# One modulation piece among every three weight pieces, in a slot of its own, and four modulation sums moved to the attention's output

## The chip, the cores and the metric

The kernel runs on one core of a Trainium2 chip. The metric is device time in microseconds of one execution, the median of several runs. The engines are TensorE (PE; its weight loads are shown apart as PEld), VectorE (DVE), ScalarE (ACT), GpSimd (POOL) and SyncE (SP), which only issues DMAs here.

## What is computed

A chain of transformer blocks on 256 tokens of width 1024, all in float32. Only the first block is touched here:

```python
mod = jax.nn.silu(c) @ w_ada[l] + b_ada[l]
sh1, sc1, g1, sh2, sc2, g2 = jnp.split(mod, 6, axis=-1)
h = modulate(rms_norm(x, norm1_g[l]), sh1, sc1)
x = x + g1[:, None, :] * token_mixer(h, w_in[l], ...)   # retention and dilated attention, gated, times w_o
h = modulate(rms_norm(x, norm2_g[l]), sh2, sc2)
x = x + g2[:, None, :] * squared_relu_mlp(h, w_ff1[l], w_ff2[l])
```

`c` is one vector of 1024, so `mod` is one row of six vectors of 1024: the scale and shift of the first norm (vectors 1 and 0), the gate of the mixer (2), the shift, scale and gate around the MLP (3, 4, 5). `w_ada` is 1024 x 6144 float32, 4 MB for each vector. The first two vectors are wanted before the first matrix product, the other four only after the mixer's last product. Behind this block come a second kind of block, twice, with mixture-of-experts layers.

## The kernel before

**Weights.** Every matrix is cut into units of 128 x 1024 float32 (512 KB). SP brings two units at a time, a piece of 1 MB, into `w_raw`, a ring of 8 unit slots, which are 4 piece slots, each with its own semaphore `raw_landed`. To keep float32 precision, ACT rounds a unit into `w_hi` (`hi`, L622), POOL takes the difference into `w_lo` (`lo`, L581, two half units of 512 columns each), and PE multiplies three times: high by high, low by high, high by low (`mm3`, L1058 to L1060). `w_hi` and `w_lo` have 4 unit slots: ACT may write unit k only when PE has used unit k-4 (`unit_used`). A unit costs PE 12 matmuls of 512 columns. Once POOL has made the difference of a unit it counts `lo_ready`, and the raw slot is free for SP.

**The stages.** Four units make a tile of the input projection (`up`, 256 tokens x 512 columns in two PSUM banks, alternately `G` and `AC`). Tiles 0 to 3 are queries and keys of the retention, 4 to 7 values, 8 to 11 its gate, and one more (`U_ATT_FIRST`, units 48 to 51) the first attention tile. While PE runs these, DVE rotates tiles 0 to 3 (`rotate`, L1854 to L1860), copies tiles 4 to 7, multiplies scores with the decay (`decayed`), normalises the four heads (`group_norm`, L1877 to L1892) and gates them (`gated`, L1897). PE puts its transposes (L1202) and the heads' scores and outputs (L1211 to L1223) between the tiles. Then comes the retention's output product (`down_pairs`, units 52 to 67, in eight pairs q with a transposition and its rounding in front of each), the attention's tiles (units 68 to 115) with the heads between units, the attention's output (116 to 119), the mixer's output (`U_WO`, 120 to 127) and the MLP (from 128).

**Modulation.** A vector of `mod` is made from 8 raw slots of `w_ada`: `ada(i, s0, s1)` has DVE multiply slot s with a column of silu(c) and add it to 128 partial rows, one SCALAR_TENSOR_TENSOR of 128 x 1024 per slot (L1802), and count `ada_used`. The sum over partitions is one product with ones on PE (`mod_sums`, L1184, into both banks of `G`), copied back by ACT (`mod_rows`, L682). In the stream, `ADA_BEFORE = (0, 0, 2, 4, 5, 8)` puts each vector as a whole round of 8 slots: vectors 0 and 1 of the order at the start, then one round before the weight rounds 2, 4, 5 and 8, that is before units 16, 32, 40 and 64. SP's loop waits, piece by piece, for `ada_used` or `lo_ready` of what stood in that slot, and issues the next. DVE works the rounds off between its other steps: vector 2 between the rotations, 3 and 4 between the group norms, 5 in the retention's output, where PE also makes the four sums (before pairs 4 to 7, `ret_head`).

**Order.** Each engine runs its own program in order; an engine waits at a semaphore and everything behind it waits too. That holds for SP's issues as well.

The trace numbers used below: a unit's steps are L622 (ACT), L581 (POOL) and L1058 to L1060 (PE).

## Time and profile before

| | before |
|---|---|
| median of 3 runs | 1512.55 us (1509.37 to 1516.2) |
| profiled execution | 1514.78 us, span 1513.0 us |
| PE busy | 1351.1 us (89%) |
| DVE busy | 854.0 us (56%) |
| ACT busy | 728.2 us (48%) |
| POOL busy | 633.0 us (42%) |
| HBM read | 274.66 MB, 184 GB/s over the span |

Busy time is how long instructions of an engine ran. The chain that ended last follows the work back from the end: an engine with a large share there is what the time hangs on in that stretch, even if its busy share over the whole span is small. POOL's 42% over the span is such a case: it makes the differences in the first half, and DVE makes them in the expert layers.

### The profile page before, as it was taken

The numbers are of one execution on the slowest core, as the hardware profiler recorded it, in microseconds if no ns is written. First come the engines' busy times: TensorE is split into PE (matmuls) and PEld (weight loads), VectorE is DVE, ScalarE is ACT, GpSimd is POOL, SyncE is SP. The second block draws the span as 40 slices with busy tenths as digits, with TensorE's granted clock in tenths as the row PEclk, the third lists the DMA queues.
The fourth block names the chain that finished last, engine by engine and source line by source line (L and its number), as shares of the span: only waits on it lengthen the run. The fifth ranks groups of instructions, "written<-read, shape, count | busy, mean of one in ns | idle before, by whom it ended". The sixth has DMA issues, their size and how long they took to land.

```text
span 1513.0 us, 18663 instructions
## 1 busy us (share of the span) xinstructions
PE 1351.1 (89%) x6112; PEld 1091.0 (72%) x6112; DVE 854.0 (56%) x1334; ACT 728.2 (48%) x1069; POOL 633.0 (42%) x525
## 2 busy tenths in 40 slices
PE   6979879999998799997987978999979888699995
PEld 2768667788876588885776767888757767678884
DVE  7463963222244543115656657777756745677777
ACT  4323354444563344443555425666635653266664
POOL 2777789787668589995300230000060024000000
PEclk8999999999998799998998878999989978699998
DMA  9765567654443445453531007778733300277782
GB/s 386 302 246 195 199 231 244 260 179 149 143 150 139 148 170 194 172 189 111 195 112 56 1 1 266 295 289 321 287 141 139 112 0 1 105 289 290 295 314 84
DMA packets 44199, 279.98 MB, mean 185 GB/s; under 512 B 5421, under 2 KB 8749, under 8 KB 11726
## 3 DMA queue, kind: packets, MB, share of 16 engines
q1 hardware_dynamic: 37138, 263.82, 47.3%
q10 hardware_dynamic: 6974, 15.05, 2.9%
q8 instruction: 48, 0.79, 0.2%
q14 instruction: 39, 0.32, 0.1%
HBM read 274.66 MB, written 4.19 MB: 184 GB/s over the span
## 4 chain that ended last, share of the span: by engine, by line
PE 39%; issue 31%; POOL 25%; DVE 3%; DVEq 1%; ACT 0%; POOLq 0%; ACTq 0%
POOL w_lo L581 23%; PE G L1058 6%; PE G L1060 6%; PE G L1059 6%; PE AC L1058 5%; PE AC L1060 5%; PE AC L1059 5%; POOL arena L606 1%; PE AC L1631 1%; PE T L1660 1%; PE G L1184 0%; DVEq L1752 0%; PE T L1274 0%; PE AC L1284 0%; DVE w_lo L1725 0%
## 5 line engine op out<-in xcount | busy, mean ns | idle before, releaser
L581 POOL TENSOR_TENSOR w_lo<-w_raw,w_hi 128x512 fp32r<-128x512 f32 (+1 forms) x488 | 608.7, 1282 | 443.2 <-ACT w_hi L622 435.8
L622 ACT ACTIVATE w_hi<-w_raw 128x1024 fp32r<-128x1024 f32 x448 | 471.1, 1059 | 412.7 <-PE G L1060 193.1
L1725 DVE TENSOR_TENSOR w_lo<-w_raw,w_hi 128x1024 fp32r<-128x1024 f32 x230 | 278.2, 1223 | 64.2 <-ACT w_hi L622 56.1
L1058 PE MATMUL G<-w_hi,xT_hi 128*128 128x512 f32 x432 | 181.9, 421 | 28.1 <-POOL w_lo L581 19.4
L1058 PE MATMUL AC<-w_hi,yT_hi 128*128 128x512 f32 x480 | 192.6, 401 | 9.8 <-POOL w_lo L581 3.9
L1059 PE MATMUL AC<-w_lo,yT_hi 128*128 128x512 f32 x480 | 189.3, 394 | 0.0
L1060 PE MATMUL AC<-w_hi,yT_lo 128*128 128x512 f32 x480 | 188.9, 393 | 0.0
L1060 PE MATMUL G<-w_hi,xT_lo 128*128 128x512 f32 x432 | 174.6, 404 | 0.0
L1059 PE MATMUL G<-w_lo,xT_hi 128*128 128x512 f32 x432 | 174.3, 404 | 0.0
L1058 PE MATMUL G<-w_hi,arena_r 128*128 128x512 f32 x320 | 128.0, 400 | 3.9 <-DVE arena L2519 3.2
L1058 PE MATMUL AC<-w_hi,xT_hi 128*128 128x512 f32 (+1 forms) x288 | 118.0, 410 | 13.2 <-DVE xT_lo L1732 7.6
L1060 PE MATMUL G<-w_hi,arena_r 128*128 128x512 f32 x320 | 125.1, 391 | 0.0
L1059 PE MATMUL G<-w_lo,arena_r 128*128 128x512 f32 x320 | 124.7, 390 | 0.0
L1058 PEld LDWEIGHTS G<-w_hi,xT_hi 128*128 128x128 f32 x432 | 85.2, 197 | 50.1 <-POOL w_lo L581 13.3
L1058 PEld LDWEIGHTS AC<-w_hi,yT_hi 128*128 128x128 f32 x480 | 92.4, 193 | 31.7 <-POOL w_lo L581 6.6
L1060 PE MATMUL AC<-w_hi,xT_lo 128*128 128x512 f32 (+1 forms) x288 | 112.8, 392 | 0.0
L1059 PE MATMUL AC<-w_lo,xT_hi 128*128 128x512 f32 (+1 forms) x288 | 112.8, 392 | 0.0
L1060 PEld LDWEIGHTS AC<-w_hi,yT_lo 128*128 128x128 f32 x480 | 92.1, 192 | 19.7
L1059 PEld LDWEIGHTS AC<-w_lo,yT_hi 128*128 128x128 f32 x480 | 92.5, 193 | 18.3
L1060 PEld LDWEIGHTS G<-w_hi,xT_lo 128*128 128x128 f32 x432 | 84.7, 196 | 19.1
L1059 PEld LDWEIGHTS G<-w_lo,xT_hi 128*128 128x128 f32 x432 | 85.5, 198 | 16.2
L606 POOL TENSOR_TENSOR arena<-arena,scr 128x256 f32<-128x256 f32 (+1 forms) x16 | 9.0, 594 | 196.4 <-ACT arena L964 196.4
(426 smaller groups left out, 1851.5 us busy)
## 6 DMA issues: line engine op xcount, KB each, us to landing
w_raw<-w_stream SPq DMA_DIRECT2D x152, 1024.0 KB, 4.8
w_raw<-w_expert SPq DMA_DIRECT2D x96, 1024.0 KB, 4.9
mod<-rows ACTq DMA_DIRECT2D x2, 2048.0 KB, 10.2
rel_scratch<-arena ACTq DMA_DIRECT2D x1, 3072.0 KB, 18.3
mod<-rows ACTq DMA_DIRECT2D x3, 476.0 KB, 5.0
x_sb<-x SPq DMA_DIRECT2D x1, 1024.0 KB, 9.4
arena<-const SPq DMA_DIRECT2D x1, 1024.0 KB, 9.6
mod<-gn_g ACTq DMA_DIRECT2D x1, 1024.0 KB, 7.3
```

Of the source, the lines that this page charges most:

```text
L581: i = pool.tensor_tensor(w_lo[:, k % SLOTS, cols], w_raw[:, k % RAW, cols], w_hi[:, k % SLOTS, cols].bitcast(F32), ALU.subtract)
L606: i = pool.tensor_tensor(sw[:, j % 4, st, a:b], sw[:, j % 4, st, a:b], cbs[j // 4][:, st * S + a:st * S + b], ALU.mult)
L622: act.activation(w_hi[:, k % SLOTS, :], w_raw[:, k % RAW, :], ACT.Copy).then_inc(hi_ready, 1)
L1058: pe.matmul(out, xh, wh, start=start, stop=False)
L1059: pe.matmul(out, xh, wl, start=False, stop=False)
L1060: return pe.matmul(out, xl, wh, start=False, stop=stop)
L1631: i = pe.matmul(AC[:, q, j * S:(j + 1) * S], x[:, t, (2 * q + j) * P:(2 * q + j + 1) * P], hot[:, t, :], start=t == 0 and x is xk_hi, stop ...
L1660: i = pe.transpose(T[:, v % 2, (2 * m + c) * P:(2 * m + c + 1) * P], moe_h[:, b, c * P:(c + 1) * P], ident[:, :])
L1725: dve.tensor_tensor(w_lo[:, k % SLOTS, :], w_raw[:, k % RAW, :], w_hi[:, k % SLOTS, :].bitcast(F32), ALU.subtract).then_inc(lo_ready, 1)
```

## The change

The first two vectors come as before. From then on, over the first 96 units (`U_MIX`), a round of four piece slots is three weight pieces (slots 0 to 5) and one modulation piece (slots 6 and 7): 16 rounds bring units 0 to 95 and the 16 pieces of the other four vectors. The ring of weights is therefore 6 units deep there instead of 8. SP waits for `lo_ready` of the same weight slot a round ago and, before a modulation piece, for `ada_used` of the piece before. From unit 96 on, the ring is as before. DVE takes the 16 pieces one at a time (`ada_piece`, two slots each): piece 0 before the first rotation, 1 after it, 2 after the third, 3 after the fourth, 4 after the second `decayed`, 5 after tile 6, 6 to 8 between the group norms and gates, 9 to 11 in the retention's output (pairs 1, 4, 7), 12 before the attention's heads, 13 to 15 among them. The four sums leave the retention's output: the first stands before the attention's output, the second before its second pair, the third and fourth before pairs 1 and 2 of the mixer's output; ACT's copies go with them. POOL's first loop is written out, since its slots are now counted modulo 6.

```diff
--- before.py
+++ after.py
@@ -75,9 +75,9 @@
 U_LAYERS = U_MLP + FF_TILES * 8
-ADA_BEFORE = (0, 0, 2, 4, 5, 8)
 ADA_ORDER = (1, 0, 2, 3, 4, 5)
-N_ADA = len(ADA_BEFORE)
+N_ADA = len(ADA_ORDER)
+U_MIX = 16 * 6
 assert KC == RAW
 L_IN = 0
@@ -170,14 +170,14 @@
     return (g, n) if n < 4 and g < len(GROUPS) else None
-def ring_round(r):
-
-    return r + sum(b <= r for b in ADA_BEFORE)
-
-
-def ada_round(i):
-
-    return i + ADA_BEFORE[i]
+def raw_slot(k):
+
+    return k % (RAW - PIECE) if k < U_MIX else k % RAW
+
+
+def raw_round(k):
+
+    return k // (RAW - PIECE) + 2 if k < U_MIX else k // RAW + N_ADA
 def program(nc, A):
@@ -515,23 +515,31 @@
                     sp.wait_ge(mod_cleared_a, 1)
                     sp.dma_start(mod[0:1, 0:2 * D], A["b_ada"][:, 0:2 * D]).then_inc(ada_b_loaded, 16)
-            rounds = sorted([(ada_round(i), "ada", i) for i in range(N_ADA)]
-                            + [(ring_round(r), "unit", r) for r in range(ADA_BEFORE[-1] + 1)])
-            for (_, kind, k), (at, _, _) in zip(rounds, rounds[1:]):
+            for s in range(n_ring):
+                sp.wait_ge(ada_used, PIECE * (s + 1))
+                piece(n_ring + s, s)
+                if s == 1:
+                    sp.dma_start(x_sb[:, :, :], A["x"].rearrange("b (t p) d -> p (b t) d", p=P)).then_inc(x_loaded, 16)
+                    sp.dma_start(W[:, 0:D], A["norm1_g"].partition_broadcast(P)).then_inc(norm1_loaded, 16)
+            sp.dma_start(ident[:, :], A["identity"]).then_inc(ident_loaded, 16)
+            for r in range(U_MIX // (RAW - PIECE)):
                 for s in range(n_ring):
-                    used = k * RAW + PIECE * (s + 1)
-                    sp.wait_ge(ada_used if kind == "ada" else lo_ready, used)
-                    piece(at * n_ring + s, s)
-                    if at == 1 and s == 1:
-                        sp.dma_start(x_sb[:, :, :], A["x"].rearrange("b (t p) d -> p (b t) d", p=P)).then_inc(x_loaded, 16)
-                        sp.dma_start(W[:, 0:D], A["norm1_g"].partition_broadcast(P)).then_inc(norm1_loaded, 16)
-                if at == 1:
-                    sp.dma_start(ident[:, :], A["identity"]).then_inc(ident_loaded, 16)
-                if at == 2:
+                    if r == 0 or s == n_ring - 1:
+                        sp.wait_ge(ada_used, RAW + PIECE * (s + 1) if r == 0 else 2 * RAW + PIECE * r)
+                    else:
+                        sp.wait_ge(lo_ready, (RAW - PIECE) * (r - 1) + PIECE * (s + 1))
+                    piece((r + 2) * n_ring + s, s)
+                if r == 0:
                     sp.dma_start(arena[:, 18432:20480], A["const1"]).then_inc(cst_loaded, 16)
...
                     sp.dma_start(pos_i[:, :], A["pos_col"]).then_inc(pos_loaded, 16)
-            with sp.Fori(ADA_BEFORE[-1] + 1, U_LAYERS // RAW) as i:
+            for s in range(n_ring):
+                if s == n_ring - 1:
+                    sp.wait_ge(ada_used, N_ADA * KC)
+                else:
+                    sp.wait_ge(lo_ready, U_MIX - (RAW - PIECE) + PIECE * (s + 1))
+                piece((U_MIX // RAW + N_ADA) * n_ring + s, s)
+            with sp.Fori(U_MIX // RAW + 1, U_LAYERS // RAW) as i:
                 for s in range(n_ring):
...
                     piece(i * n_ring + (N_ADA * n_ring + s), s)
@@ -575,10 +583,11 @@
             pool.memset(mod[:, 2 * D:], 0.0).then_inc(mod_cleared_b, 1)
             def lo(n, k, width):
+                raw = raw_slot(k) if isinstance(n, int) else k % RAW
                 pool.wait_ge(hi_ready, n + (k + 1))
...
                     cols = slice(a, a + width)
-                    i = pool.tensor_tensor(w_lo[:, k % SLOTS, cols], w_raw[:, k % RAW, cols],
+                    i = pool.tensor_tensor(w_lo[:, k % SLOTS, cols], w_raw[:, raw, cols],
                                            w_hi[:, k % SLOTS, cols].bitcast(F32), ALU.subtract)
                 i.then_inc(lo_ready, 1)
@@ -586,7 +595,9 @@
                 for s in range(RAW):
                     lo(n, s, width)
-            with pool.Fori(0, U_ATT_OUT // RAW) as i:
+            for k in range(U_MIX):
+                lo(0, k, UNIT // 2)
+            with pool.Fori(U_MIX // RAW, U_ATT_OUT // RAW) as i:
                 lo_round(i * RAW, UNIT // 2)
...
                 if k == U_ATT_OUT:
@@ -614,12 +625,12 @@
             def hi(n, k):
                 if isinstance(n, int):
-                    landed = (ring_round((n + k) // RAW) + 1) * 16
+                    raw, landed = raw_slot(n + k), (raw_round(n + k) + 1) * 16
                 else:
-                    landed = n * (16 // RAW) + (k // RAW + N_ADA + 1) * 16
-                act.wait_ge(raw_landed[k % RAW // PIECE], landed)
+                    raw, landed = k % RAW, n * (16 // RAW) + (k // RAW + N_ADA + 1) * 16
+                act.wait_ge(raw_landed[raw // PIECE], landed)
                 act.wait_ge(unit_used, n + k + 1)
-                act.activation(w_hi[:, k % SLOTS, :], w_raw[:, k % RAW, :], ACT.Copy).then_inc(hi_ready, 1)
+                act.activation(w_hi[:, k % SLOTS, :], w_raw[:, raw, :], ACT.Copy).then_inc(hi_ready, 1)
             def his(a, b, n=0):
                 for k in range(a, b):
@@ -728,11 +739,6 @@
             act.wait_ge(y_ready, RH)
             act.wait_ge(bias_stored, 16)
-            def mod_and_bias(q):
-                if 2 * RH - (N_ADA - 2) <= q < 2 * RH:
-                    mod_rows(q - 2 * RH + N_ADA)
-                load_bias(q)
-
             def load_bias(q):
                 g = q // 2
@@ -745,7 +751,7 @@
                     act.dma_start(rel[g][:, :, c0:c0 + n], src).then_inc(rel_loaded[g], 16)
-            down_his(0, U_RET_OUT, T_RET, 2 * RH, mod_and_bias)
+            down_his(0, U_RET_OUT, T_RET, 2 * RH, load_bias)
             his(U_ATT_IN + SLOTS, POS0 - UP + SLOTS)
             n_turned = 0
@@ -784,8 +790,9 @@
             his(U_ATT_OUT - 1 + SLOTS, U_ATT_OUT + SLOTS)
...
             act.dma_start(norm2_row, A["norm2_g"].partition_broadcast(P)).then_inc(norm2_loaded, 16)
-            down_his(0, U_ATT_OUT, T_ATT, 2)
-            down_his(0, U_WO, T_MERGE, 4)
+            mod_rows(2)
+            down_his(0, U_ATT_OUT, T_ATT, 2, lambda q: mod_rows(3) if q == 0 else None)
+            down_his(0, U_WO, T_MERGE, 4, lambda q: mod_rows(4 + q) if q < 2 else None)
             act.dma_start(arena[:, 17024:17664], A["const2"]).then_inc(cst2_loaded, 16)
...
             act.dma_start(slot_iota, A["slot_iota"].partition_broadcast(P)).then_inc(cst2_loaded, 16)
@@ -1252,12 +1259,9 @@
             def ret_head(q):
                 pe.wait_ge(y_ready, q // 2 + 1)
-                if q >= 2 * RH - (N_ADA - 2):
-                    pe.wait_ge(g_free, G_CREDIT + M_ATT_IN + 1)
-                    mod_sums(q - 2 * RH + N_ADA)
             down_pairs(0, U_RET_OUT, T_RET, lambda q: tile(8 + q // 2)[:, :, q % 2 * 256:(q % 2 + 1) * 256], 2 * RH, ret_head)
-            pe.wait_ge(mod_out, N_ADA)
+            pe.wait_ge(g_free, G_CREDIT + M_ATT_IN + 1)
             up(0, U_ATT_IN, G)
             pe.wait_ge(acc_free, 1)
@@ -1324,14 +1328,28 @@
                 if head_at(p, 4) is not None:
                     att_values(head_at(p, 4))
+            pe.wait_ge(gate_read, N_GATE - 1)
+            mod_sums(2)
             pe.wait_ge(att_ready, 1)
             pe.wait_ge(ao_out, N_AH)
-            down_pairs(0, U_ATT_OUT, T_ATT, lambda q: tile(0)[:, :, q * 256:(q + 1) * 256], 2,
-                       lambda q: pe.wait_ge(gate_read, N_GATE - 1 + q))
+
+            def att_head(q):
+
+                if q == 1:
+                    pe.wait_ge(gate_read, N_GATE)
+                    mod_sums(3)
+
+            def merged_head(q):
+
+                if 1 <= q <= 2:
+                    mod_sums(3 + q)
+                pe.wait_ge(merged_ready, q // 2 + 1)
+
+            down_pairs(0, U_ATT_OUT, T_ATT, lambda q: tile(0)[:, :, q * 256:(q + 1) * 256], 2, att_head)
             pe.wait_ge(acc_free, 2)
-            down_pairs(0, U_WO, T_MERGE, lambda q: tile(10 + q // 2)[:, :, q % 2 * 256:(q % 2 + 1) * 256], 4,
-                       lambda q: pe.wait_ge(merged_ready, q // 2 + 1))
-
+            down_pairs(0, U_WO, T_MERGE, lambda q: tile(10 + q // 2)[:, :, q % 2 * 256:(q % 2 + 1) * 256], 4, merged_head)
+
+            pe.wait_ge(mod_out, N_ADA)
             up_normed(0, U_MLP, G, T_H2, h_sb, h_ready, 2)
...
             clear_acc()
@@ -1798,8 +1816,10 @@
                 v = ADA_ORDER[i]
...
                 for s in range(s0, s1):
-                    dve.wait_ge(raw_landed[s // PIECE], 16 * (ada_round(i) + 1))
-                    dve.scalar_tensor_tensor(m, w_raw[:, s, :], csil[:, s:s + 1], m, ALU.mult, ALU.add).then_inc(ada_used, 1)
+                    q = (i * KC + s) // PIECE - 2 * (RAW // PIECE)
+                    raw, landed = (s, i) if i < 2 else (RAW - PIECE + s % PIECE, 2 + q)
+                    dve.wait_ge(raw_landed[raw // PIECE], 16 * (landed + 1))
+                    dve.scalar_tensor_tensor(m, w_raw[:, raw, :], csil[:, s:s + 1], m, ALU.mult, ALU.add).then_inc(ada_used, 1)
                     dep()
...
                     dve.memset(sm[:, 892:893], 0.0).then_inc(ada_summed, 1)
@@ -1896,44 +1916,56 @@
                 dve.wait_ge(rg_gated, h + 1)
                 dve.tensor_tensor(tile(8 + h), tile(8 + h), tile(h), ALU.mult).then_inc(y_ready, 1)
+            def ada_piece(q):
+
+                ada(2 + q * PIECE // KC, q * PIECE % KC, q * PIECE % KC + PIECE)
+
             dve.wait_ge(ada_b2_loaded, 16)
-            for j in range(4):
-                rotate(j)
-                if j in (1, 2):
-                    ada(2, 4 * j - 4, 4 * j)
+            ada_piece(0)
+            rotate(0)
+            ada_piece(1)
+            rotate(1)
+            rotate(2)
+            ada_piece(2)
+            rotate(3)
+            ada_piece(3)
             ret_in_tile(4)
...
             decayed(1)
+            ada_piece(4)
             ret_in_tile(6)
-            ada(3, 0, 4)
+            ada_piece(5)
             group_norm(0)
...
             ret_in_tile(7)
-            ada(3, 4, KC)
             group_norm(1)
             decayed(3)
-            ada(4, 0, 4)
+            ada_piece(6)
             group_norm(2)
             gated(0)
-            ada(4, 4, KC)
+            ada_piece(7)
             group_norm(3)
...
             gated(3)
+            ada_piece(8)
             read_tile(tile(0), G, done(U_ATT_FIRST + UP))
...
                 down_los(T_RET, q, q + 1)
-                if 2 <= q < 6:
-                    ada(5, 2 * (q - 2), 2 * (q - 1))
+                if q in (1, 4, 7):
+                    ada_piece(9 + q // 3)
             acc_ct = AC[:, :, :].rearrange("p (t c) n -> p t c n", t=TOK)
...
             read_tile(tile(1), G, done(U_ATT_IN + UP))
+            ada_piece(12)
             for p in range(-UP, N_POS):
+                if p in (2, 8, 14):
+                    ada_piece(13 + p // 6)
                 k = head_at(p, 3)
...
                     dve.wait_ge(aeT_ready, k + 1)
@@ -2615,8 +2647,11 @@
         router = np.concatenate([a["router_group_w_2"][l], we], axis=1)
...
     units = np.concatenate(parts, axis=0).reshape(-1, RAW, P, UNIT)
-    ada = a["w_ada"][0].reshape(KC, P, N_ADA, D).transpose(2, 0, 1, 3)
-    units = np.insert(units, ADA_BEFORE, ada[list(ADA_ORDER)], axis=0)
+    ada = a["w_ada"][0].reshape(KC, P, N_ADA, D).transpose(2, 0, 1, 3)[list(ADA_ORDER)]
+    units, ada = units.reshape(-1, PIECE, P, UNIT), ada.reshape(-1, PIECE, P, D)
+    first, n_first = 2 * RAW // PIECE, U_MIX // PIECE
+    mixed = np.concatenate([units[:n_first].reshape(-1, RAW // PIECE - 1, PIECE, P, UNIT), ada[first:, None]], axis=1)
+    units = np.concatenate([ada[:first], mixed.reshape(-1, PIECE, P, UNIT), units[n_first:]], axis=0)
     return by_piece(units)
```

## Rows read from the trace of the kernel before

**Rows 1.** Page, parts 4 and 5: the chain by line; POOL's half units (x count).

```profile
POOL w_lo L581 23%; PE G L1058 6%; PE G L1060 6%; PE G L1059 6%; PE AC L1058 5%; PE AC L1060 5%; PE AC L1059 5%; POOL arena L606 1%; PE AC L1631 1%; PE T L1660 1%; PE G L1184 0%; DVEq L1752 0%; PE T L1274 0%; PE AC L1284 0%; DVE w_lo L1725 0%
L581 POOL TENSOR_TENSOR w_lo<-w_raw,w_hi 128x512 fp32r<-128x512 f32 (+1 forms) x488 | 608.7, 1282 | 443.2 <-ACT w_hi L622 435.8
```

**Rows 2.** Waits, 40 to 300 us: total us, times, longest us.

```profile
POOL w_lo L581 <- ACT w_hi L622: 49.2, 16, 8.4
ACT w_hi L622 <- DMA w_raw<-w_stream: 31.3, 7, 15.6
```

**Rows 3.** Timeline of PE: start us, us, instruction, idle before and its releaser.

```profile
68.77 0.47 PE L1058 MATMUL G<-w_hi,xT_hi 128*128 128x512 f32 x1
...
79.78 1.03 PE L1202 MATMUL T<-ident,arena 128*128 128x128 f32 x8
80.67 0.47 PE L1058 MATMUL AC<-w_hi,xT_hi 128*128 128x512 f32 x1
...
93.33 1.04 PE L1202 MATMUL T<-ident,arena 128*128 128x128 f32 x8
101.45 0.77 PE L1058 MATMUL G<-w_hi,xT_hi 128*128 128x512 f32 x1 [7.09 <-POOL w_lo L581]
...
125.55 1.02 PE L1211 MATMUL T<-arena 128*128 128x256 f32 x4
...
128.08 0.48 PE L1058 MATMUL G<-w_hi,xT_hi 128*128 128x512 f32 x1
...
139.06 1.02 PE L1221 MATMUL AC<-arena,scr 128*128 128x512 f32 x2
...
142.86 0.48 PE L1058 MATMUL AC<-w_hi,xT_hi 128*128 128x512 f32 x1
...
170.69 1.02 PE L1221 MATMUL AC<-arena,scr 128*128 128x512 f32 x2
...
172.87 0.79 PE L1058 MATMUL AC<-w_hi,xT_hi 128*128 128x512 f32 x1
...
187.75 1.02 PE L1221 MATMUL AC<-arena,scr 128*128 128x512 f32 x2
...
196.86 0.77 PE L1058 MATMUL G<-w_hi,xT_hi 128*128 128x512 f32 x1 [6.37 <-POOL w_lo L581]
...
233.69 0.60 PE L1141 MATMUL T<-ident,arena 128*128 128x128 f32 x4
```

**Rows 4.** Line L581 in 97:120 and in 140:186: ns minimum/median/maximum.

```profile
L581 POOL TENSOR_TENSOR w_lo<-w_raw,w_hi x17: 1272/1290/1739, 98.8 to 119.7; 128x512 fp32r<-128x512 f32 x17
...
L581 POOL TENSOR_TENSOR w_lo<-w_raw,w_hi x19: 1267/2251/2349, 139.0 to 183.6; 128x512 fp32r<-128x512 f32 x19
```

**Rows 5.** Timeline of DVE: modulation products and a group norm's step.

```profile
91.06 2.66 DVE L1802 SCALAR_TENSOR_TENSOR mod<-w_raw,sm,mod 128x1024 f32<-128x1024 f32 x2
...
155.55 8.39 DVE L1802 SCALAR_TENSOR_TENSOR mod<-w_raw,sm,mod 128x1024 f32<-128x1024 f32 x4
...
169.17 2.16 DVE L1890 TENSOR_TENSOR arena<-arena,mod 128x1024 f32<-128x1024 f32 x1
```

**Rows 6.** Timeline of POOL: units 4 to 15.

```profile
54.09 36.32 POOL L581 TENSOR_TENSOR w_lo<-w_raw,w_hi 128x512 fp32r<-128x512 f32 x24 [7.81 <-ACT w_hi L622]
```

**Rows 7.** Page, part 6: DMA issues, KB each, median us to landing.

```profile
w_raw<-w_stream SPq DMA_DIRECT2D x152, 1024.0 KB, 4.8
...
rel_scratch<-arena ACTq DMA_DIRECT2D x1, 3072.0 KB, 18.3
```

**Rows 8.** Timeline of PE: one modulation sum; the mixer's output before the change.

```profile
253.73 1.88 PE L1184 MATMUL G<-mod,sm 128*128 128x512 f32 x4
...
470.24 1.09 PE L1141 MATMUL T<-ident,arena 128*128 128x128 f32 x4 [4.52 <-issue]
...
473.04 0.78 PE L1058 MATMUL AC<-w_hi,yT_hi 128*128 128x512 f32 x1
...
480.16 0.60 PE L1141 MATMUL T<-ident,arena 128*128 128x128 f32 x4
```

## Prediction, made before the changed kernel ran

> **What bounds the kernel now.** I read the chain of work that ended last first. Its largest share is not PE but POOL's L581, 23% of the span [rows 1], though POOL is busy for only 42% of it. So in part of the kernel the difference of each unit, not the product, sets the pace. The stretch is 54 to 234 us: POOL's timeline has units 4 to 15 back to back, 24 half units in 36.3 us without a pause [rows 6]. Then it stops: between 40 and 300 us POOL waits 49.2 us for ACT, and ACT's own long waits are for weight pieces, 31.3 us, one of 15.6 [rows 2]. Those are the rounds in which all eight raw slots hold modulation and no weight can be on its way.
>
> What it costs is read on PE. A tile of four units takes 79.78 - 68.77 = 11.0 us at the full clock (2.75 a unit). The joints between tiles take 0.9 (a transposition, 80.67 - 79.78), 2.5 (two heads' scores, 128.08 - 125.55), 3.8 (a head's output and scores, 142.86 - 139.06) and 2.2 (an output, 172.87 - 170.69) [rows 3]. From 68.77 to 233.69 there are 11 tiles, three joints of 0.9, one of 2.5, two of 3.8, two of 2.2: 121.0 + 17.2 = 138.2. It took 164.9, so 26.7 us are lost. Two gaps carry 14.1: 101.45 - 93.33 less 0.9 is 7.2, and 196.86 - 187.75 less 2.2 is 6.9 [rows 3]. The other 12.6 is spread over tiles whose differences come late, and over matmuls at the lower clock behind a gap.
>
> Why differences come late: a half unit takes POOL 1.27 to 1.29 us, but its median is 2.25 where DVE multiplies modulation and normalises [rows 4], so 1.0 more. DVE pays too: 1.33 us a product with POOL idle (2.66 for two), 2.1 beside it (8.39 for four) [rows 5]. POOL's undisturbed unit, 2.54, against PE's 2.75 leaves it 0.2 a unit to catch up. So each modulation product of DVE beside a busy POOL is a debt of 1.0 us. An operation of DVE that reads PSUM (L1854 to L1857, the tile copies) leaves POOL at 1.3; one with two SBUF inputs does not: one in a rotation (0.9 in all), the two 128 x 1024 steps of a group norm (2.16 each instead of 1.23 [rows 5], 2.1 for POOL), the gate product (1.0).
>
> The Trainium skill says why ("SBUF — State Buffer", section "Who interferes with whom"): a DVE instruction with two SBUF inputs and a GpSimd instruction that reads SBUF share a port, and the later one fully blocks until the first is done. This speaks against the change, which moves modulation products from POOL's pauses to its busy time; taken literally each would cost POOL DVE's whole 1.33, not 1.0, and the ledger below, with some 14 such operations on the binding path, would end 4 to 5 us later.
>
> **The change part by part.**
>
> *Ring.* No round is without weights any more, so both long gaps go. A weight piece of round r+1 is issued when POOL has done unit 6r+1, lands 4.8 us later [rows 7] and is wanted by POOL four units on, 10.2 us of its work: 4 us to spare after ACT's 1.1. The shallower ring alone costs nothing. Queued behind SP's new wait for `ada_used` are the next weight pieces: the sums of piece q must be done by 4 us after POOL's unit 6q+7. In the ledger DVE finishes each of them 4 us or more before that, so I take nothing; the price if not is a rival.
>
> *DVE and POOL, tile by tile.* POOL's end of a tile is its last end + 10.2 + debts (2.0 a piece, 0.9 a rotation, 2.1 a norm, 1.0 a gate product), but it can run only four units ahead of PE. PE's end is its start + 11.0, or POOL's end + 2.7 if later. Piece 0 waits for the bias store (issued at 36.2, 18.3 us [rows 7]), so it starts at 54.5, just as POOL starts unit 4 [rows 6]; before, nothing stood there. POOL has no lead in tile 1, so this is paid at once.
> Tile 1: POOL 54.1 + 10.2 + 2.9 = 67.2, PE 69.9 (before 68.0). Tile 2 (rotation, piece 1): 80.3, 83.0. Tile 3 (rotation, most of piece 2): 92.7, 95.4. Tile 4 (rest, rotation): 104.5, 107.3. Tile 5 (piece 3): 116.7, 119.4. Tile 6 (piece 4): 128.9, 132.9; from here the joints of 2.5 and 3.8 give POOL a lead. Tiles 7 and 8 (piece 5, norm 0): PE sets the time, 147.7, 162.5. Tile 9 (norm 1, piece 6): 169.6, 175.7. Tile 10 (norm 2, gate 0, part of piece 7): 183.7, 188.9. Tile 11 (rest, norm 3, gate 1): 198.2, 200.9. Last tile (gates 2 and 3, piece 8): 198.2 + 10.2 + 4.0 = 212.4, PE 215.1. Against 233.69 this gives **18.6 us**. If the debts cost nothing, the bound is 26.7 plus nothing; if POOL is held 1.3 each and norms 3.0, it is about 12. I take the ledger, since its 1.0 is the row of just this pair.
>
> *Retention's output.* Four sums leave it: one takes 1.88 by its row [rows 8], 1.7 to the next transposition: **7.0 us** gained, since PE has no wait there. Pieces 9 to 11 now come in pairs 1, 4 and 7; DVE needs 4.4 us for one beside POOL, a pair has 5.9, and DVE's 0.8 for the rounding must fit too. If a piece lands badly the rounding is 0 to 1.5 us late. Three pieces: **-0.7**, range 0 to -4. POOL's debt of 2.0 each is hidden by 0.4 a unit of slack there.
>
> *Attention.* Pieces 12 to 15 give POOL 8 us of debt over 24 units in which PE takes 3.2 to 3.8 with its heads against 2.54: hidden. If DVE delays a head's scores, by some 1 us twice, they are wanted three units later: hidden. 0, range 0 to -3.
>
> *The four sums at their new place.* The first two stand before and inside the attention's output, where PE waits for POOL's units 116 to 119, which start only when DVE's combination of the heads is done: 0, if that cover were gone 3.4. ACT's copies, 1.0 each, stand in front of the roundings there, also hidden. The third comes at 470.24, behind a PE idle of 4.5 us, at the lower clock: twice 1.7, so 3.4. But there PE waited 1 us for the second rounding, and units 120 and 121 took 480.16 - 473.04 = 7.1 [rows 8] instead of 5.6 because of the same low clock, which now falls on the sum: net 1.1. The fourth stands before pair 2 with nothing to hide it: 1.7. ACT's copy of it now waits in front of the rounding of units 124 and 125; these come 2.7 us late against 6 us of work that PE has: hidden. Together **-2.8**; ends: 0 if waits cover them, -7 if all show.
>
> *Code.* POOL's and SP's loops written out: nothing, at most 1 either way; instruction DMA is 0.3% of the engines' time.
>
> *Sum.* 18.6 + 7.0 - 0.7 - 2.8 = **22.1 us**. Everything behind the mixer hangs on chip events, not on absolute time, so the shift is passed on. The profiled execution took 1514.78 (span 1513.0); less 22.1 is 1492.7. The median shown is 2.2 lower than that execution, so 1490.5; I say **1491**.
>
> **The rivals.**
> (A) *The debt is heavier than the ledger*: POOL is the bound in nearly all of 54 to 215 us, norms and products never fall in a pause, and PE falls to the lower clock in the small gaps. Gain 12 before the retention's output, 7 - 2 there, -5 later: 12 us, 1500. For it: tile 9 took 14.9 us instead of 11.0 (172.87 to 187.75) with no missing weight [rows 3]. Against: the ledger has that already.
> (B) *The debt is lighter*: DVE gives way more often than POOL. 26.7 + 7 - 2 = 31, 1481. For it: DVE's product stretches by 0.8 as well, so the pair shares. Against: POOL's median of 2.25 [rows 4].
> (C) *Slower: SP's queue is blocked by DVE.* Every weight piece of a round now stands behind a wait for DVE's last piece, and DVE's pieces stand behind its waits for PE, rotation and norms. If each of some 12 rounds is late by more than its 4 us, the loss comes again in each, and a piece that lands late holds the rotation or norm behind it. To be over 0.5% slower it must cost 22 + 8 = 30 us, 2.5 us in each of 12 rounds, so each piece 6.5 us later than the ledger has it: 1522. Against: the ledger has 4 us or more in hand, most often over 10.
> (D) *The order doesn't do what it says*: weights are there in time but POOL simply loses in its busy time what it lost in pauses (the four vectors' 32 products at 1.0 = 32 us, against 27 lost now): gain 7 from the sums less 3, 1508. Against: before, about half the products ran beside POOL already, so at most 16 more are added, and those in the attention are hidden.
>
> **How the numbers follow.** Forecast 0.62 (1484 to 1498), A 0.16, B 0.10, C 0.05, D 0.07. Range 1481 to 1503: A's and B's values are in, C and D are out. 0.5% is 7.6 us and about what a measurement here can tell from no change. Faster: forecast, A, B: 0.88. Same: D and a little of A: 0.08. Slower: 0.04.
>
> **What would show it.** PE's waits of 7.09 and 6.37 for POOL gone, and no wait of ACT for a weight piece over 3 us. POOL without a pause over 2 us from 54 us to the end of the retention's tiles, with more of its half units at 2.25. The retention's output's first transposition near 215. No L1184 in it, and 5.9 us a pair. The attention's tiles as long as before. PE at the mixer's output 3 us longer. It is wrong if SP's waits for DVE (L1802) are followed by waits of ACT for pieces, if tiles 1 to 4 together are over 4 us later than in the ledger, or if the attention's heads take longer.

## The result, and the profile after

| | before | after |
|---|---|---|
| median, same session | 1514.38 us (1509.37 to 1516.97) | 1503.28 us (1501.3 to 1505.56) |
| ratio after / before | | 0.9932, 95% interval 0.9908 to 0.9957 |
| profiled execution | 1514.78 us, span 1513.0 | 1505.56 us, span 1503.7 |

The change gains 0.7%, half of the 22.1 us that I forecast, and the time lies just above the range's 1503. The page of after, its chain by line and the groups of POOL's differences (L590 here, L581 before) and DVE's modulation products (L1822 here, L1802 before):

```profile
POOL w_lo L590 23%; PE G L1065 6%; PE G L1067 6%; PE G L1066 6%; PE AC L1065 5%; PE AC L1067 5%; PE AC L1066 5%; DMA w_raw<-w_stream 1%; DVE mod L1822 1%; POOL arena L617 1%; ACT w_hi L633 1%; PE T L1678 1%; PE AC L1649 1%; DVEq L1770 0%; DVE w_lo L1743 0%
...
L590 POOL TENSOR_TENSOR w_lo<-w_raw,w_hi 128x512 fp32r<-128x512 f32 (+1 forms) x488 | 616.0, 1299 | 421.0 <-ACT w_hi L633 413.7
```

POOL's share of the chain is 23% as in [rows 1], but three entries are new: a DMA of raw weights, DVE's modulation products and ACT's rounding (L633), with 1% each. The shares don't say who waits for whom; the waits do. Those of after, all engines, 40 to 300 us (engine and what it waited for: us in all, times, longest):

```profile
DVE mod L1822 <- DMA w_raw<-w_stream: 39.9, 10, 10.9
POOL w_lo L590 <- ACT w_hi L633: 34.2, 9, 10.8
ACT sm L661 <- DVE sm L1761: 33.5, 4, 13.6
PE AC L1065 <- POOL w_lo L590: 9.4, 1, 9.4
```

ACT's waits for weight pieces, 31.3 us and one of 15.6 in [rows 2], are gone but for one of 1.9. POOL still waits 34.2 us for ACT's rounding against 49.2, with one wait of 10.8, and this time ACT isn't short of weights: it waits for DVE, before the square root of a group norm (L661). DVE waits 39.9 us for landings of modulation pieces.

To place the difference I take the start of the first product of a unit in PE's timeline (L1065; L1058 before) as a mark, and read four stretches: A, unit 4 to unit 52 (the tiles of the first projection); B, unit 52 to 68 (the retention's output); C, unit 68 to 116 (the attention's tiles); D, unit 116 to the MLP's first transposition (both output products).

| us | A | B | C | D | sum |
|---|---|---|---|---|---|
| before | 179.5 | 53.7 | 162.7 | 51.8 | 447.7 |
| forecast for after | 160.9 | 47.4 | 162.7 | 54.6 | 425.6 |
| after | 172.2 | 46.5 | 164.5 | 52.3 | 435.5 |

The forecast's row takes off 18.6 in A and 7.0 less 0.7 in B, and adds 2.8 in D. Measured: -7.3, -7.2, +1.8, +0.5, together -12.2. Outside of these stretches after took 1.1 us more up to unit 4 and 1.9 more from the MLP to the last product. Such parts, in which nothing was changed, scatter by some us from one profiled execution to the next (over the kernels below, 56.7 to 60.1 us to unit 4, and 790.5 to 799.1 us from the last unit of the dense feed-forward part to the last product). So I compare stretches where a whole time would say too little. Each stretch is read from one profiled execution: where two or three kernels have the same program in A, their A differs by 1.0 to 1.8 us (172.2, 171.2 and 170.4 in the order of the change), and B by up to 1.1, so differences of one or two us say nothing by themselves. The missing 9.9 us are an A that is 11.3 too long, less 0.9 in B and 0.5 in C and D together.

Where in A? PE's timeline of after (start, us, line, what, [idle before <- released by]):

```profile
163.41 0.79 PE L1065 MATMUL AC<-w_hi,xT_hi 128*128 128x512 f32 x1
...
179.40 0.47 PE L1065 MATMUL G<-w_hi,xT_hi 128*128 128x512 f32 x1 [1.94 <-POOL w_lo L590]
...
201.53 0.76 PE L1065 MATMUL AC<-w_hi,xT_hi 128*128 128x512 f32 x1 [9.38 <-POOL w_lo L590]
215.44 0.39 PE L1065 MATMUL G<-w_hi,xT_hi 128*128 128x512 f32 x1
226.33 0.60 PE L1148 MATMUL T<-ident,arena 128*128 128x128 f32 x4
```

The waits of 7.09 and 6.37 in [rows 3] are gone, but there is a new one of 9.38 before unit 44. The tile from 179.40 took 22.1 us. The ends of PE's tiles against the ledger (last product of each four units, from the same timeline):

| tile | 1 | 2 | 3 | 4 | 5 | 6 | 7 | 8 | 9 | 10 | 11 | last |
|---|---|---|---|---|---|---|---|---|---|---|---|---|
| ledger | 69.9 | 83.0 | 95.4 | 107.3 | 119.4 | 132.9 | 147.7 | 162.5 | 175.7 | 188.9 | 200.9 | 215.1 |
| after | 69.2 | 82.1 | 94.0 | 106.2 | 118.3 | 131.8 | 146.6 | 161.4 | 174.9 | 192.2 | 215.6 | 226.5 |

Up to tile 9 the ledger is right within 1.4 us. Then it misses by 3.3, 14.7 and 11.4. (Unit 4 itself began 1.1 us later than before; counted from there, the ledger is up to 2.5 us too long in tiles 1 to 9, and misses by 2.2, 13.6 and 10.3 behind them.)

**The new wait, read backwards.** The chain of waits of after, cut to 176 to 202 us (start, us, engine and line):

```profile
175.40 6.35 POOL w_lo L590 x4
...
181.76 0.33 SPq L507
...
182.13 6.91 DMA w_raw<-w_stream
...
189.06 1.28 DVE mod L1822
...
190.44 1.28 DVE mod L1822
...
193.77 0.18 DVE sm L1761
193.97 0.03 ACT sm L661
...
194.19 1.28 ACT L738
...
196.41 1.06 ACT w_hi L633
...
197.53 3.87 POOL w_lo L590 x2
...
201.53 0.76 PE AC L1065
```

POOL ends unit 41 at 181.74. That frees a slot, SP issues the round's third weight piece and, right behind it, modulation piece 7, which lands 6.9 us later. DVE multiplies it, and only then begins norm 3, whose variance ACT's root wants. Behind the root (and a silu, L738) in ACT's order stands the rounding of unit 44, behind that POOL's difference, behind that PE. The rows of the two engines that stood still, DVE and ACT:

```profile
175.99 2.14 DVE L1917 TENSOR_TENSOR arena<-arena 128x1024 f32<-128x1024 f32 x1
189.06 2.66 DVE L1822 SCALAR_TENSOR_TENSOR mod<-w_raw,sm,mod 128x1024 f32<-128x1024 f32 x2 [10.93 <-DMA w_raw<-w_stream]
```

```profile
193.97 0.20 ACT L661 ACTIVATE sm<-sm 128x2 f32<-128x2 f32 x1 [13.61 <-DVE sm L1761]
```

So POOL can't go on before DVE has had piece 7, and piece 7 can't be issued before POOL has done unit 41. Between the end of unit 41 and the start of unit 44 lie 15.8 us, in which POOL has two units of work, 5.1 us.

### The profile page after: what moved, and what is told of

Its sections match the earlier page's. It is cut to its first block, busy times and chain, and to the rows that moved or that the text cites. A ratio compares the mean times of both kernels' runs of the same rounds, so it can differ in the third digit from the quotient of the medians.

```text
span 1503.7 us, 18463 instructions
## 1 busy us (share of the span) xinstructions
PE 1353.9 (90%) x6112; PEld 1094.2 (73%) x6112; DVE 858.5 (57%) x1334; ACT 727.4 (48%) x1069; POOL 640.4 (43%) x525
## 4 chain that ended last, share of the span: by engine, by line
PE 40%; issue 26%; POOL 24%; DVE 5%; DVEq 2%; DMA 2%; ACT 2%; POOLq 0%; SPq 0%; ACTq 0%
POOL w_lo L590 23%; PE G L1065 6%; PE G L1067 6%; PE G L1066 6%; PE AC L1065 5%; PE AC L1067 5%; PE AC L1066 5%; DMA w_raw<-w_stream 1%; DVE mod L1822 1%; POOL arena L617 1%; ACT w_hi L633 1%; PE T L1678 1%; PE AC L1649 1%; DVEq L1770 0%; DVE w_lo L1743 0%
## 5 line engine op out<-in xcount | busy, mean ns | idle before, releaser
L590 POOL TENSOR_TENSOR w_lo<-w_raw,w_hi 128x512 fp32r<-128x512 f32 (+1 forms) x488 | 616.0, 1299 | 421.0 <-ACT w_hi L633 413.7
L633 ACT ACTIVATE w_hi<-w_raw 128x1024 fp32r<-128x1024 f32 x448 | 471.2, 1059 | 387.5 <-PE G L1067 193.8
L1065 PE MATMUL AC<-w_hi,yT_hi 128*128 128x512 f32 x480 | 190.7, 397 | 9.8 <-POOL w_lo L590 4.0
L1065 PE MATMUL G<-w_hi,xT_hi 128*128 128x512 f32 x432 | 180.8, 419 | 13.5 <-DVE xT_lo L1750 8.1
L1065 PE MATMUL AC<-w_hi,xT_hi 128*128 128x512 f32 (+1 forms) x288 | 118.9, 413 | 17.9 <-POOL w_lo L590 9.4
L1065 PE MATMUL G<-w_hi,arena_r 128*128 128x512 f32 x320 | 128.0, 400 | 4.6 <-DVE arena L2551 3.2
L1065 PEld LDWEIGHTS AC<-w_hi,yT_hi 128*128 128x128 f32 x480 | 91.4, 190 | 31.4 <-POOL w_lo L590 6.6
L1065 PEld LDWEIGHTS G<-w_hi,xT_hi 128*128 128x128 f32 x432 | 84.8, 196 | 35.9 <-POOL w_lo L590 12.0
L1822 DVE SCALAR_TENSOR_TENSOR mod<-w_raw,sm,mod 128x1024 f32<-128x1024 f32 x48 | 81.1, 1690 | 44.4 <-DMA w_raw<-w_stream 41.3
```

Of the source, the lines that this page charges most:

```text
L590: i = pool.tensor_tensor(w_lo[:, k % SLOTS, cols], w_raw[:, raw, cols], w_hi[:, k % SLOTS, cols].bitcast(F32), ALU.subtract)
L633: act.activation(w_hi[:, k % SLOTS, :], w_raw[:, raw, :], ACT.Copy).then_inc(hi_ready, 1)
L1065: pe.matmul(out, xh, wh, start=start, stop=False)
L1822: dve.scalar_tensor_tensor(m, w_raw[:, raw, :], csil[:, s:s + 1], m, ALU.mult, ALU.add).then_inc(ada_used, 1)
```

## The experiments

The theory after the result, "chain": the piece in front of a norm costs some 10 us of A, by way of ACT's order. The rival, "port": A is long because POOL loses more beside DVE than the ledger has. All ratios are to before in the same session.

**Piece 7 behind norm 3.**

```
 gated(0)
-ada_piece(7)
 group_norm(3)
+ada_piece(7)
 gated(1)
```

> The changed kernel with modulation piece 7 taken behind the group norm of head 3 instead of before it. Theory (the chain): in the changed kernel DVE stood 10.9 us waiting for piece 7, the norm of head 3 behind it, ScalarE's square root behind the norm (13.6 us idle) and its rounding of unit 44 behind the root, so TensorE's tile 11 began at 201.5 instead of about 190. With the norm first, tile 11 begins 9 to 11 us earlier and the kernel takes 1492 to 1494 us (0.985 to 0.988 of before). Rival (the port): the loss is GpSimd's slowed differences; the order of one piece and one norm does not matter: 1501 to 1504 us.

Measured: 1492.3 us, ratio 0.9883 (0.9853 to 0.9912). A took 162.7 us against 172.2, so 9.5 less. PE's timeline of this kernel at the same tiles:

```profile
179.21 0.47 PE L1065 MATMUL G<-w_hi,xT_hi 128*128 128x512 f32 x1 [2.13 <-POOL w_lo L590]
...
191.81 0.39 PE L1065 MATMUL AC<-w_hi,xT_hi 128*128 128x512 f32 x1
...
205.86 0.39 PE L1065 MATMUL G<-w_hi,xT_hi 128*128 128x512 f32 x1
```

The tile takes 12.6 us instead of 22.1, with no wait before unit 44. Two lines exchanged in DVE's program, which take no work away, give back 9.5 of the 11.3 us that A was too long: the chain is shown. When DVE comes to piece 7 now, at 190.27, the piece has landed, and it doesn't wait.

**Pieces 5, 6 and 7 behind norms 0, 2 and 3** (piece 7 as above).

```
-ada_piece(5)
 group_norm(0)
+ada_piece(5)
 ...
-ada_piece(6)
 group_norm(2)
+ada_piece(6)
```

> The changed kernel with pieces 5, 6 and 7 each behind the group norm they stood before (heads 0, 2 and 3). Theory (the chain): piece 6 cost 2.5 us in front of tile 10 and piece 5 only GpSimd's lead, so 2 to 4 us below the kernel with piece 7 alone moved: 1489 to 1491 us. Rival (the port): no different from the changed kernel, 1501 to 1504 us.

Measured: 1490.12 us, 0.9856 (0.9833 to 0.9878). A took 161.6 us, the ledger's 160.9 within 0.7. The wait of 2.13 before the tile at 179 is gone too, and ACT waits 10.1 us in all for DVE before its four roots, at most 3.2, against 33.5 and 13.6. In B this execution took 54.0 us where after took 46.5: DVE waited 7.2 us for piece 9, the pair of products behind that took 7.8 us beside POOL instead of 4.4 (below, in the part on the hardware), and the rounding behind both was late. It isn't paid every time: the profiled execution took 1496.53 us, the other three 1489.91 to 1490.13.

**Products of 8 columns instead of 1024**, for the four late vectors; the order is that of the change.

```
-dve.scalar_tensor_tensor(m, w_raw[:, raw, :], csil[:, s:s + 1], m, ALU.mult, ALU.add)
+w = D if i < 2 else 8
+dve.scalar_tensor_tensor(m[:, 0:w], w_raw[:, raw, 0:w], csil[:, s:s + 1], m[:, 0:w], ALU.mult, ALU.add)
```

> The changed kernel with VectorE's 32 products for the last four modulation vectors cut to 8 columns each; all pieces still land and all waits stay. Left out: most of the sums of those four vectors, so the output is not the reference's. Theory (the chain): the wait for piece 7 to land stays (it is issued when GpSimd has done unit 42), so the gap before tile 11 shrinks only by the 2.7 us of the two products; in all 4 to 7 us come back: 1496 to 1499 us. Rival (the port): GpSimd is no longer held, and 12 to 15 us come back: 1488 to 1491 us.

Measured: 1488.94 us, 0.9863 (0.9821 to 0.9904), where the chain alone expected 1496 to 1499 and the port 1488 to 1491. Against the chain? PE's timeline says that it is still there:

```profile
173.84 0.79 PE L1065 MATMUL G<-w_hi,xT_hi 128*128 128x512 f32 x1
...
192.11 0.77 PE L1065 MATMUL AC<-w_hi,xT_hi 128*128 128x512 f32 x1 [6.80 <-POOL w_lo L590]
```

The tile takes 18.3 us, so the chain isn't gone, and the whole time alone would have pointed to the port. So both causes are real: A falls from 172.2 to 161.9 us with the order left as it is, and to 161.6 with the products left as they are. What each is worth beside the other, the next run tells. I had counted the products' part too small.

**Short products and pieces behind the norms**, both edits together.

> Both at once: the 32 products cut to 8 columns, and pieces 5, 6 and 7 behind the norms (output not the reference's). If the loss has two parts that add up, the chain through the landing of piece 7 (7.3 us were left in front of tile 11 with short products) and VectorE's products themselves, this is 6 to 8 us below the kernel with short products alone, 1481 to 1483 us, and no tile of the retention takes more than 11.4 us. Rival: the two runs found the same microseconds twice; then 1487 to 1489 us.

Measured: 1486.58 us, 0.9835 (0.9808 to 0.9862). By whole time only 2.4 us below the last one (4 by the ratios, whose intervals overlap), where over 5 were expected; by stretch A is 155.4, which is 6.5 below the short products alone and 6.2 below the norms first alone. The four stretches together took 418.6 us against 425.2; what is missing in the whole time is scatter outside of them. Together the two edits take 16.8 us out of A, alone 10.6 (order) and 10.3 (products): they overlap by 4, about what the long tile lost when the products were short (22.1 to 18.3). With the norms first, the products' debt in A is **6.2 us**. The nine pieces of A hold POOL for 18 by the ledger's 2.0 each; the other two thirds lie in its lead.

**The sums moved alone**, on the kernel before with its whole rounds: `mod_sums` and `mod_rows` as in the change, the ring and its waits as they were.

> The kernel before with only the four sums moved from the retention's output to the attention's and the mixer's output; the ring is the old one. The sums leave 7.0 us in the retention's output and cost 2 to 3 in their new place: 4 to 5 us faster than before, 1509 to 1511 us, if the old ring's rounds leave that stretch as it is. Rival: the old ring's round before unit 64 is then what sets the time there (ScalarE waited 7.5 us for a weight piece under the sums), and only 0 to 2 us are left.

Measured: 1512.72 us, 1.0011 (0.9993 to 1.0029): no change, which is what the rival had. B took 52.2 us, 1.5 less than before, though the four sums' 7 us are out of it. Its waits in B (236 to 292 us):

```profile
DVE mod L1809 <- DMA w_raw<-w_stream: 11.5, 4, 6.5
...
PE T L1137 <- DVE yT_lo L1726: 5.4, 4, 1.8
```

DVE takes its eight slots of the last vector in B in the old ring, waits for their landings, and the roundings that the transpositions want stand behind that. The sums had been hiding it: with them out, PE waits 5.4 us instead of 1.6. The rival had named ACT's wait for a weight piece; it is there, 9.5 us long, but PE waits only 1.4 us in all for POOL in this stretch, so that isn't the path. C and D pay 3.6 for the sums at their new place. So the move of the sums brings its 7 us only with the new ring: the two halves of the change are not independent.

**No late sums.** `mod_sums(2)` to `(5)` and `mod_rows(2)` to `(5)` left out.

> The changed kernel with the four late sums and ScalarE's four copies of them left out (so the last four vectors stay 128 partial rows and the output is not the reference's). It prices them at their new place: from TensorE's first transposition of the attention's output to the last four units of the mixer's output the changed kernel took 1.8 us more than before (38.9 against 37.1) and 0.7 more behind that. Theory (a third of the prediction's price, mostly hidden): 2 to 4 us below the changed kernel, 1499 to 1501. Rival (the copies and the blocked rounding cost more than the trace shows): 6 us or more, 1497 or less.

Measured: 1496.22 us, 0.9901 (0.988 to 0.9922), by the ratios 5 us under after. By its whole time this is the rival's value, but it isn't all the sums' doing: A, which the edit doesn't touch, took 170.4, and from the MLP to the last product it took 989.2 us against 996.7. C was 162.6 and D 52.1, against after's 164.5 and 52.3. So the sums cost 2.1 us by stretch, the theory's 2 to 4.

**Norms first, pieces of B one pair later, third and fourth sum in PE's pause.** The kernel with pieces 5, 6 and 7 behind the norms, and three more edits:

```
-if q in (1, 4, 7):
+if q in (2, 5, 7):
     ada_piece(9 + q // 3)
...
-if 1 <= q <= 2:
-    mod_sums(3 + q)
...
 down_pairs(0, U_ATT_OUT, ...)
+mod_sums(4)
+mod_sums(5)
 pe.wait_ge(acc_free, 2)
```

> Pieces 5, 6, 7 behind the norms, pieces 9 to 11 in pairs 2, 5 and 7 of the retention's output instead of 1, 4 and 7, and the third and fourth late sums in TensorE's pause between the attention's output and the mixer's output. With the norms first alone TensorE lost 1.6 us (in one execution 7.5) in pair 2, because VectorE stood 6.6 us waiting for piece 9 with the pair's rounding behind it; the two sums cost 1.8 us net in the changed kernel. Theory: 3 to 4 us below the kernel with pieces behind norms: 1486 to 1488 us. Rival: DVE's waits only move to other pairs and the pause is too short for two sums and two copies: 1489 to 1492 us.

Measured: 1484.63 us, 0.9822 (0.9796 to 0.9848). A 160.5, B 46.5, C 164.5, D 48.4: 420.0 in all, and the best kernel here, by the ratios 1.1% below the changed one. D is 3.9 us shorter than after's and even 3.7 shorter than without sums. PE's timeline shows the two sums in the pause before the mixer's output:

```profile
441.32 1.88 PE L1193 MATMUL G<-mod,sm 128*128 128x512 f32 x4
...
444.40 1.95 PE L1193 MATMUL G<-mod,sm 128*128 128x512 f32 x4 [1.21 <-ACT mod L693]
446.19 0.60 PE L1150 MATMUL T<-ident,arena 128*128 128x128 f32 x4
```

**The modulation piece third, not last, in its round.** The order of the change, with SP's issues exchanged:

```
-for s in range(n_ring):
+for s in range(n_ring) if r == 0 else (0, 1, 3, 2):
```

> The changed kernel with SP's order in a round changed alone: the modulation piece is issued before the third weight piece instead of behind it, so it goes out two units earlier (about 5 us) and lands alone (4.7 instead of 6.9 us). Theory (VectorE waits for the landing with a norm behind): the wait of 10.9 us for piece 7 shrinks by about 7, tile 11 begins 6 to 8 us earlier, the kernel takes 1493 to 1497 us. Rival (the weight pieces, now 2 us later and behind one more wait, become the bound): 1502 us or more.

Measured: 1489.1 us, 0.9855 (0.9834 to 0.9875), lower than the theory had. A 162.6, B 46.6. Its waits, 40 to 300 us:

```profile
POOL w_lo L590 <- ACT w_hi L633: 21.4, 11, 7.5
...
ACT sm L661 <- DVE sm L1761: 11.6, 4, 3.3
```

and DVE waits for landings 2.9 us in all instead of 39.9. The piece no longer stands behind the weight piece that needs POOL's unit 41, only behind the one that needs unit 39. The loop through POOL is still there, but with two units of slack, and that is enough here. One line in SP's order does nearly what moving three pieces in DVE's does (A 161.6), and B stays at after's length. The weight piece, now behind it, costs ACT one wait of 3.2 us.

**Both**: the edits of the best kernel and SP's order.

> The order of e7 (pieces behind the norms, later pieces in pairs 2, 5, 7, two sums in the pause) together with SP's order of e8 (modulation piece before the third weight piece). If what each takes away is the same wait of VectorE for a landing, the two don't add up in the retention's tiles: 0 to 3 us below e7, 1482 to 1485 us; the rest there is the price of the products themselves (6 us, by e6). Rival: the weight pieces behind the earlier wait come late and it is slower than e7, over 1487 us.

Measured: 1485.64 us, 0.983 (0.9807 to 0.9853), just above the expected range and no better than 1484.63: both edits cut the same chain. A was 163.8 us, 3.3 more than in the best kernel. Most of this arises before tile 6, which starts 65.1 us behind unit 4 instead of 62.7, and so it does in the kernel with SP's order alone. The largest part, 1.9 us, is in tile 4: piece 3 lands earlier, and DVE's two products follow the fourth rotation at once (100.0 us) instead of 5 us later, so that both of their debts fall into one tile in which POOL has no lead. A piece can come too early for POOL too.

**Debt moved out of A**: the best kernel, with piece 7 behind the last gate and pieces 8 to 11 in B, at pairs 1, 3, 5 and 7.

> e7 with piece 7 behind the last gate product and pieces 8 to 11 in pairs 1, 3, 5, 7 of the retention's output, where GpSimd has 0.4 us a unit to spare, instead of pieces 7 and 8 beside the last norm and gates. Theory of the debt (1.0 us of GpSimd a product): TensorE's last three retention tiles, 11 + 3.4 and 11 + 0.7 and about 3 in front of the first pair in e7, lose 2 to 4 us: 1481 to 1483 us. Rival: VectorE's pieces in four pairs instead of three make the pairs' roundings late, and it comes out the same or slower, 1484 to 1488.

Measured: 1488.81 us, 0.986 (0.9834 to 0.9887), by the ratios 0.4% slower than the best, which the intervals don't tell apart. By stretch A 164.0, B 49.0, both longer, 6.1 us in all. The chain of waits, 208 to 223 us, and ACT's row in it:

```profile
210.40 2.16 DVE mod L1824
...
212.58 0.33 SPq L507
...
212.95 7.07 DMA w_raw<-w_stream
...
222.35 0.44 DVE yT_lo L1739
...
222.92 1.09 PE T L1150 x4
```

```profile
220.04 1.06 ACT L633 ACTIVATE w_hi<-w_raw 128x1024 fp32r<-128x1024 f32 x1 [9.16 <-DMA w_raw<-w_stream]
```

DVE now comes to piece 7 at 208. SP stands at its wait for `ada_used` until 212.56, the weight piece behind it lands 7.1 us later, and ACT's rounding, DVE's and PE's transposition, idle for 5.74 us, follow. This is the mechanism of rival C, which the change itself doesn't show: a piece that is taken too late stops the weights, one that is asked for too early stops the norms. The 6.2 us of debt can't be had this way.

**The changed kernel again**, in the session of the last two:

> The changed kernel once more, unchanged, beside the two above, to see how far its time and the lengths of its unchanged stages (up to unit 4, and behind the MLP) move from one execution to the next. 1500 to 1505 us; from unit 4 to the first transposition of the MLP 435 to 437 us, as in its first profile.

Measured: 1502.57 us (1498.11 to 1507.49), 0.9932 (0.9909 to 0.9954), A 171.2, the four stretches 436.7. The result stands.

## Why the prediction was wrong, point by point

**The sign and the place were right, the size was half.** 12.2 us by stretch where 22.1 were forecast.

**Ring and its waits: wrong, and this is the step that failed.** I put the new waits at nothing: "the sums of piece q must be done by 4 us after POOL's unit 6q+7. In the ledger DVE finishes each of them 4 us or more before that, so I take nothing." I asked only whether DVE would be late for SP, not whether the piece would be late for DVE. Piece 7 is issued behind POOL's unit 41; DVE had nothing else to do from 178.1 and waited 10.93. Rival C named the thing in half a sentence, "a piece that lands late holds the rotation or norm behind it", but priced it for every round and for SP. And the norm was not late for DVE's own sake: the path to PE went through ACT's root to the rounding of the next weight unit. What I had put at nothing was worth 9.5 us for piece 7 and 10.6 for pieces 5, 6 and 7 (A 172.2, then 162.7 and 161.6), of the 11.3 that A was too long. The trace of before had this row, in the same view as [rows 2], and I didn't use it:

```profile
ACT sm L650 <- DVE sm L1743: 30.1, 4, 10.7
```

ACT already stood up to 10.7 us before a root. What I named as a sign, no wait of ACT for a weight piece over 3 us, came true, and said nothing on this.

**DVE and POOL, tile by tile: right in the main.** 1.0 us a half unit and 2.0 a piece, POOL at most four units ahead, and the joints gave A's tile ends within 1.4 us up to tile 9, and A as a whole within 0.7 us once norms stood first (161.6 against 160.9). A price of 1.33 us a product, which the prediction put at 4 to 5 us more, isn't borne out. That the whole agrees so well is in part luck: counted from unit 4, the kernel with the norms first is up to 1.6 us ahead of the ledger through tile 10, and ends tile 11, in which a norm's steps, a piece and two gate products follow each other, 3.3 us behind it. POOL's half units between 140 and 186 us, after:

```profile
L590 POOL TENSOR_TENSOR w_lo<-w_raw,w_hi x24: 1277/1296/2273, 145.2 to 185.4; 128x512 fp32r<-128x512 f32 x24
```

Minimum and maximum are about those of [rows 4], so a half unit loses no more beside DVE than it did. With A at the ledger's length once the chain is cut, rival A, a heavier debt, and B, a lighter one, are both out, though after's 1503 lies nearest to A's 1500: the number would have been good for a reason that isn't there. Rival D, that the order does nothing, is out too: it had 1508 us, a ratio of 0.997, against 0.9932 (to 0.9957), and A gained 7.3 us.

**Retention's output: right.** 7.2 us for a forecast of 6.3. The 0.7 for the three pieces wasn't paid in after; the kernel with the norms first paid 7.5 there once. It holds only together with the new ring (1.5 us alone).

**Attention: right.** Without sums C took 162.6 us against 162.7 before, with four pieces more in it: POOL's debt is hidden there.

**The four sums: the total right, the terms wrong.** Forecast 2.8, measured 2.1 by leaving them out, 2.3 against before. But I gave the first two 0 and the last two 2.8. PE's timeline of after:

```profile
435.75 1.88 PE L1191 MATMUL G<-mod,sm 128*128 128x512 f32 x4
...
438.98 1.96 PE L1191 MATMUL G<-mod,sm 128*128 128x512 f32 x4 [0.91 <-ACT mod L693]
...
456.88 1.09 PE L1148 MATMUL T<-ident,arena 128*128 128x128 f32 x4 [4.55 <-issue]
457.75 3.15 PE L1191 MATMUL G<-mod,sm 128*128 128x512 f32 x4
...
466.65 1.88 PE L1191 MATMUL G<-mod,sm 128*128 128x512 f32 x4
```

The first stands before unit 116 where PE came without a pause, and delays the transposition behind it by 1.7 us, nearly all of C's growth: no cover. The second stands where PE without it waits 2.15 us for DVE's rounding, and adds some 0.5. The third costs 3.15 at the lower clock, as said, and the fourth 1.88, yet D grew by 0.2 to 0.5 only: what the units behind lose to the clock without them is as large. Units 120 to 123 in the three kernels, by windows (first the kernel changed, then without sums, then with them in the pause; window and its length, busy us and instructions of PE, PEld, DVE, ACT and POOL, granted clock of PE, DMA share, GB/s):

```profile
461.10:474.60 13.50, 13.50 (x62) 10.51 (x60) 1.51 (x4) 5.89 (x10) 3.98 (x4) 1.00 0.18 72
```

```profile
460.90:474.40 13.50, 13.50 (x58) 11.02 (x57) 1.60 (x4) 4.58 (x8) 6.76 (x6) 0.87 0.32 97
```

```profile
448.70:460.60 11.90, 11.90 (x60) 9.87 (x58) 1.51 (x4) 4.53 (x8) 6.85 (x7) 1.00 0.34 112
```

With a sum among them they take the same 13.5 us as without it, at a granted clock of 1.00 (the upper level all through) instead of 0.87 (part of the stretch at the lower); with both sums in the idle time ahead, 11.9.

**Code and the rest: nothing**, as far as the scatter of the untouched parts lets one see.

## What to carry to other kernels

When a transfer is made to come at a fixed place in a queue, ask both ways: who waits for it if it is late, and what its own issue waits for. If the engine that takes it is ahead of work on which the slot's release depends, the two close a loop, and an engine with slack on paper (DVE here) sets the pace through a third one's order (ACT's root in front of a weight's rounding). It is cheap to cut: the step that others wait for goes first, or the piece is issued before the one with the later condition. A step that is moved away may have been hiding another wait (the sums alone gave 1.5 of 7 us), and work put into a matmul engine's pause can be worth more than its own time.

## What the runs showed of the hardware that I had not expected

**Who waits for the port.** Products of 8 columns beside POOL's half units (the kernel with short products, POOL's and DVE's timelines):

```profile
157.49 4.99 POOL L590 TENSOR_TENSOR w_lo<-w_raw,w_hi 128x512 fp32r<-128x512 f32 x4
```

```profile
157.64 2.38 DVE L1823 SCALAR_TENSOR_TENSOR mod<-w_raw,sm,mod 128x8 f32<-128x8 f32 x2 [0.56 <-DMA w_raw<-w_stream]
```

Two of them take 0.54 with POOL idle (at 181.75) and 2.38 here, about 1.2 each, while POOL's four half units keep their 1.25. DVE's short product here ends about when POOL's half unit does, however little it has to do itself, and POOL loses nothing that can be read. This is the lock that the Trainium skill states ("SBUF — State Buffer", "Who interferes with whom"), and here the trace agrees with it better than for full products, where a half unit takes 2.25 us beside a product, which is less than 1.27 plus 1.33.

**A piece behind a piece.** The median landing of a piece of 1 MB is 4.8 us [rows 7]; modulation piece 7, issued 0.4 us behind a weight piece, took 6.9. It is no accident of this piece: in after's trace all 12 pieces that SP issued 0.37 us behind another between 60 and 300 us took 6.7 to 8.4 us to land, and the pieces just ahead of them 4.6 to 4.8. In the chain above this is 2 of the 10 us.

**POOL can keep the port.** Some operations of DVE take far longer than 2.2 us: a gate product of after, and one of the pair of modulation products in the kernel with the norms first. From their DVE timelines:

```profile
217.70 5.70 DVE L1917 TENSOR_TENSOR arena<-arena 128x1024 f32<-128x1024 f32 x1 [15.23 <-ACT arena L738]
```

```profile
227.55 7.80 DVE L1822 SCALAR_TENSOR_TENSOR mod<-w_raw,sm,mod 128x1024 f32<-128x1024 f32 x2 [7.18 <-DMA w_raw<-w_stream]
```

The same take 2.14 (at 175.99) and 4.4. In after, POOL's half units during this time, up to 222.2 us and then (min, median, max; first and last start):

```profile
L590 POOL TENSOR_TENSOR w_lo<-w_raw,w_hi x5: 1322/1328/1352, 216.0 to 221.0; 128x512 fp32r<-128x512 f32 x5
```

```profile
L590 POOL TENSOR_TENSOR w_lo<-w_raw,w_hi x3: 1352/2262/2277, 221.0 to 224.5; 128x512 fp32r<-128x512 f32 x3
```

While DVE's operation waits, POOL's half units follow each other undelayed, and the first long one is that at 222.28, as DVE gets through (the next, at 224.51, stands beside DVE's next operation). In the second kernel three half units from 228.3 take 1.28 to 1.30 before one takes 2.23. PE then waited 5.2 us for DVE and ran at the lower clock behind it, and B lost 7.5 us; with piece 7 alone moved, DVE waited as long for piece 9 (6.6 us) but its pair took 4.7, and B lost 1.7. So the loser may have to wait for several instructions of the other, not one; before I had taken them to alternate. This is read from two traces; no run was made to bring it about or prevent it, and why POOL keeps the port here and not elsewhere stays open.
